# Two of the four weight sums of a paired step computed on GpSimd

## What is computed

```
def swiglu(x, w_gate, w_up, w_down):
    return (jax.nn.silu(x @ w_gate) * (x @ w_up)) @ w_down
...
        f = swiglu(rms_norm_2(x, g[0]), ffn_w_gate[layer, 0], ffn_w_up[layer, 0], ffn_w_down[layer, 0])
        x = x + 0.5 * rms_norm_2(f, g[1])
```

## Time and profile before

| | us |
|---|---|
| median of 3 runs (1793.16 to 1794.82) | 1794.06 |
| the profiled execution | 1793.34 |
| its span, from the first to the last instruction | 1790.4 |
| TensorE busy | 1754.3 |
| VectorE busy | 1389.7 |
| ScalarE busy | 995.0 |
| GpSimd busy | 58.1 |

### The profile page before, as it was taken

The page is one execution under the profiler, slowest core; times in us unless marked ns, Lnnn a source line. Parts: engine busy times, 40 slices in busy tenths (PEclk is TensorE's granted clock), DMA queues, the critical chain, the costliest instruction groups (busy, mean ns, idle before and its releaser), DMA issues.

```text
span 1790.4 us, 25225 instructions
## 1 busy us (share of the span) xinstructions
PE 1754.3 (98%) x10314; PEld 1482.6 (83%) x10314; DVE 1389.7 (78%) x1646; ACT 995.0 (56%) x1206; POOL 58.1 (3%) x98
## 2 busy tenths in 40 slices
PE   9999999999999999999999999999999999999998
PEld 8998898888888887787898988778877878787877
DVE  5349877788898898978498779886897667879784
ACT  5446653577777676645452355555555456656453
POOL 0040000000000001000000000000100010010000
PEclk9999999999999999999999999999999999999999
DMA  9343344699899897373442016527443745234631
GB/s 383 118 165 136 119 148 149 240 359 351 337 351 354 334 372 293 123 280 139 190 152 108 27 53 230 225 83 312 180 170 136 305 143 187 72 141 150 273 147 76
DMA packets 51379, 363.01 MB, mean 203 GB/s; under 512 B 5697, under 2 KB 5825, under 8 KB 8642
## 3 DMA queue, kind: packets, MB, share of 16 engines
q1 hardware_dynamic: 50976, 359.24, 52.6%
q10 hardware_dynamic: 290, 2.17, 0.3%
HBM read 360.34 MB, written 1.05 MB: 202 GB/s over the span
## 4 chain that ended last, share of the span: by engine, by line
PE 79%; DVE 15%; ACT 3%; issue 1%; DMA 1%; POOL 0%; DVEq 0%; POOLq 0%; ACTq 0%
PE bank L2866 8%; PE bank L3424 4%; PE bank L3426 4%; PE bank L3425 4%; PE bank L3451 3%; PE bank L3449 3%; PE bank L3450 3%; PE bank L3278 3%; PE bank L3280 3%; PE bank L3279 3%; DVE w_a L1718 3%; PE bank L3483 3%; PE bank L2924 3%; PE bank L3484 2%; PE bank L3485 2%; PE bank L3295 2%
## 5 line engine op out<-in xcount | busy, mean ns | idle before, releaser
L1718 DVE TENSOR_TENSOR w_a<-ring,w_a 128x2048 fp32r<-128x2048 f32 x220 | 500.4, 2287 | 132.5 <-ACT w_a L994 131.8
L994 ACT ACTIVATE w_a<-ring 128x2048 fp32r<-128x2048 f32 x219 | 416.2, 1913 | 121.4 <-PE bank L3451 42.1
L1718 DVE TENSOR_TENSOR w_b<-ring,w_b 128x2048 fp32r<-128x2048 f32 x63 | 144.1, 2287 | 29.3 <-ACT w_b L994 29.2
L994 ACT ACTIVATE w_b<-ring 128x2048 fp32r<-128x2048 f32 x63 | 120.5, 1912 | 36.2 <-PE bank L3426 17.8
L2866 PE MATMUL bank<-h,w_a 128*128 128x256 f32 x1040 | 137.3, 285 | 1.0 <-DVE ring_lo L1823 1.0
L2866 PEld LDWEIGHTS bank<-h,w_a 128*128 128x128 f32 x1040 | 128.8, 191 | 4.1 <-issue 3.0
L3449 PE MATMUL bank<-w_a,hid 128*128 128x512 f32 x280 | 109.9, 393 | 0.0
L3451 PE MATMUL bank<-w_a,hid 128*128 128x512 f32 x280 | 109.2, 390 | 0.0
L3450 PE MATMUL bank<-w_a,hid 128*128 128x512 f32 x280 | 109.0, 389 | 0.0
L3424 PE MATMUL bank<-w_a,h 128*128 128x512 f32 x240 | 95.0, 396 | 0.5 <-DVE w_a L1718 0.5
L3426 PE MATMUL bank<-w_a,h 128*128 128x512 f32 x240 | 93.7, 390 | 0.0
(11 more groups left out here) (648 smaller groups left out, 4201.1 us busy)
## 6 DMA issues: line engine op xcount, KB each, us to landing
ring<-in_stream SPq DMA_DIRECT2D x330, 1024.0 KB, 5.3
G<-in_gains SPq DMA_DIRECT2D x14, 512.0 KB, 7.8
cmp_area<-in_cmp_w ACTq DMA_DIRECT2D x1, 2048.0 KB, 11.3
sm<-in_small SPq DMA_DIRECT2D x1, 1582.0 KB, 12.0
con<-in_consts SPq DMA_DIRECT2D x1, 1032.0 KB, 15.9
X<-in_x SPq DMA_DIRECT2D x2, 512.0 KB, 4.0
out_x<-X SPq DMA_DIRECT2D x4, 256.0 KB, 2.0
sm<-in_small SPq DMA_DIRECT2D x1, 730.5 KB, 22.5
```

The costliest lines, as they stand in the source:

```text
L994: act.activation(w_slot(unit)[:, 0, :], ring[:, unit % RING, :], ACT.Copy).then_inc(S("w_hi"), 1)
L1718: dve.tensor_tensor(w_slot(unit)[:, 1, :], ring[:, unit % RING, :], w_slot(unit)[:, 0, :].bitcast(FP32), ALU.subtract).then_inc(S("w_lo"), 1)
```

## The change

t3 and t1 move to GpSimd, which runs its own `weight_sums` in each network: t3 as soon as b12 and b22 have landed. t1 is now computed inside the pair, as b22 - t2 (t2 is b22 - b12 + b11), when t2 is made and m6 is done. VectorE's t2 waits for GpSimd's t3. The high half of t1 on ScalarE waits for GpSimd's t1, and so does the load into b11's place, which followed m6 before; the load into b22's place waits for t1 too. The low half of t2 is written to `w_sum_lo` (the tile `y_2`) instead of `ring_lo`. GpSimd's count is kept in the semaphore `ffn_pool`, in which the sparse network's steps count first (`m_silu` before).

```diff
--- before.py
+++ after.py
@@ -668,9 +668,10 @@
...
-        PAIR_DVE = ["t1", "t3", "t2", "t4", "t2_lo", "u2", "t4_lo", "u3", "c21", "t1_lo", "w", "c12", "c22"]
+        PAIR_DVE = ["t2", "t4", "t2_lo", "u2", "t4_lo", "u3", "c21", "t1_lo", "w", "c12", "c22"]
         FFN_DVE = ["x_raw", "s1", "s2", "s3", "s4", "s_lo"] + [f"{step}_{i}" for i in range(len(PAIRS)) for step in PAIR_DVE]
         FFN_ACT = ["s_hi"] + [f"{step}_{i}" for i in range(len(PAIRS)) for step in ("t2_hi", "m1", "t4_hi", "t1_hi")]
+        FFN_POOL = [f"{step}_{i}" for i in range(len(PAIRS)) for step in ("t3", "t1")]
         FFN_PE = [f"{step}_{i}" for i in range(len(PAIRS)) for step in ("m6", "m7", "m4", "m5")]
 
         def ffn_at(steps, name, step):
@@ -737,10 +738,12 @@
                 return "sums_0", NB[name] - (NB[name] > NB["ffn0"])
             return "unit_used", D_UNITS[of] + (3 * STEPS[of] if of in STEPS else SQUARE)
 
+        SUMMED = {}
         for name in FFNS:
             for i, s in enumerate(PAIRS):
-                b11, b21, _, _ = pair_units(name, s)
-                RELEASE[b11] = ("ffn_pe", ffn_at(FFN_PE, name, f"m6_{i}"))
+                b11, b21, _, b22 = pair_units(name, s)
+                SUMMED[b22] = ffn_at(FFN_POOL, name, f"t1_{i}")
+                RELEASE[b11] = ("ffn_pool", ffn_at(FFN_POOL, name, f"t1_{i}"))
                 RELEASE[b21] = ("ffn_pe", ffn_at(FFN_PE, name, f"m4_{i}"))
 
         def tops_done(name, s):
@@ -818,6 +821,8 @@
                 if u >= RING:
                     name, count = RELEASE.get(u - RING, ("unit_used", u - RING + 1))
                     sp.wait_ge(S(name), count)
+                    if u - RING in SUMMED:
+                        sp.wait_ge(S("ffn_pool"), SUMMED[u - RING])
                 sp.dma_start(ring[:, u % RING, :], unit_at(u)).then_inc(S(f"unit{u % RING}"), 16)
 
             def load_gain(row, place):
@@ -939,18 +944,33 @@
                 src, dst = dst, src
 
 
+            def weight_sums(name):
+                for i, s in enumerate(PAIRS):
+                    b11, _, b12, b22 = pair_units(name, s)
+                    for b in (b12, b22):
+                        pool.wait_ge(S(f"unit{b % RING}"), 16 * (b // RING + 1))
+                    pool.tensor_tensor(ring[:, b12 % RING, :], ring[:, b22 % RING, :], ring[:, b12 % RING, :], ALU.subtract)\
+                        .then_inc(S("ffn_pool"), 1)
+                    pool.wait_ge(S("ffn_dve"), ffn_at(FFN_DVE, name, f"t2_{i}"))
+                    pool.wait_ge(S("ffn_pe"), ffn_at(FFN_PE, name, f"m6_{i}"))
+                    pool.tensor_tensor(w_sum, ring[:, b22 % RING, :], ring[:, b11 % RING, :], ALU.subtract).then_inc(S("ffn_pool"), 1)
+
             post_power("moe")
-            for name in ("ffn0", "ab"):
-                post_power(name)
+            post_power("ffn0")
+            weight_sums("ffn0")
+            post_power("ab")
...
-            for name in ("ffn1", "ffn2", "c"):
+            for name in ("ffn1", "ffn2"):
                 post_power(name)
-            for name in ("ffn3", "end"):
-                post_power(name)
+                weight_sums(name)
+            post_power("c")
+            post_power("ffn3")
+            weight_sums("ffn3")
+            post_power("end")
 
 
         @block.scalar
@@ -1348,7 +1368,7 @@
                     if s == 0:
                         act.wait_ge(S("route_dve"), AT["rc_ok"])
                     act.wait_ge(S("unit_used"), m0 + place_A("moe", s) + 2)
-                    act.activation(sil_m[:, :], bank[4][:, 0:UC], ACT.Silu, scale=rc[:, 6 * i + 4:6 * i + 5]).then_inc(S("m_silu"), 1)
+                    act.activation(sil_m[:, :], bank[4][:, 0:UC], ACT.Silu, scale=rc[:, 6 * i + 4:6 * i + 5]).then_inc(S("ffn_pool"), 1)
                     if s:
                         split_at(3 * s + 3)
                     act.wait_ge(S("ffn_pe"), s + 1)
@@ -1412,6 +1432,7 @@
                     act.wait_ge(S("unit_used"), b21 + 1)
                     silu_of(bank[4], 0)
                     split_at(3 * s + 4)
+                    act.wait_ge(S("ffn_pool"), ffn_at(FFN_POOL, name, f"t1_{i}"))
                     act.wait_ge(S("ffn_pe"), ffn_at(FFN_PE, name, f"m4_{i}"))
                     act.activation(sum_hi[:, :], w_sum, ACT.Copy).then_inc(S("ffn_act"), 1)
                     act.wait_ge(S("ffn_dve"), ffn_at(FFN_DVE, name, f"c21_{i}"))
@@ -2296,7 +2317,7 @@
 
                 for s in range(SPARSE_STEPS):
                     i, j = s // GRP_STEPS, s % GRP_STEPS
-                    dve.wait_ge(S("m_silu"), s + 1)
+                    dve.wait_ge(S("ffn_pool"), s + 1)
                     e = 6 * i + j // 2
                     dve.scalar_tensor_tensor(mid_m[:, s % 2, :], bank[4][:, UC:2 * UC], rc[:, e:e + 1], sil_m[:, :], ALU.mult, ALU.mult)\
                        .then_inc(S("ffn_dve"), 1)
@@ -2361,20 +2382,10 @@
                     own("s2")
                     dve.tensor_tensor(x_sum[:, 3], a12, x_sum[:, 1], ALU.subtract).then_inc(S("ffn_dve"), 1)
 
-                def weight_sums(i, s):
-                    b11, b21, b12, b22 = pair_units(name, s)
-                    raw = [ring[:, b % RING, :] for b in (b11, b21, b12, b22)]
-                    if i:
-                        dve.wait_ge(S("ffn_pe"), ffn_at(FFN_PE, name, f"m5_{i - 1}"))
-                    dve.wait_ge(S(f"unit{b11 % RING}"), 16 * (b11 // RING + 1))
-                    dve.wait_ge(S(f"unit{b12 % RING}"), 16 * (b12 // RING + 1))
-                    dve.tensor_tensor(w_sum, raw[2], raw[0], ALU.subtract).then_inc(S("ffn_dve"), 1)
-                    dve.wait_ge(S(f"unit{b22 % RING}"), 16 * (b22 // RING + 1))
-                    dve.tensor_tensor(raw[2], raw[3], raw[2], ALU.subtract).then_inc(S("ffn_dve"), 1)
-
                 def more_weight_sums(i, s):
                     b11, b21, b12, _ = pair_units(name, s)
-                    own(f"t3_{i}")
+                    dve.wait_ge(S("ffn_pool"), ffn_at(FFN_POOL, name, f"t3_{i}"))
+                    dve.wait_ge(S(f"unit{b11 % RING}"), 16 * (b11 // RING + 1))
                     dve.tensor_tensor(ring[:, b11 % RING, :], ring[:, b12 % RING, :], ring[:, b11 % RING, :], ALU.add).then_inc(S("ffn_dve"), 1)
                     own(f"t2_{i}")
                     dve.tensor_tensor(ring[:, b21 % RING, :], ring[:, b21 % RING, :], ring[:, b11 % RING, :], ALU.subtract)\
@@ -2440,13 +2451,11 @@
                     hid_left(s - 1, range(0, 2))
                     if s + 2 == PAIRS[0]:
                         x_whole()
-                    if ahead is not None:
-                        weight_sums(ahead, s + 1)
                     split_at(3 * s + 3)
                     hid_made(s, 1)
                     if ahead is not None:
                         more_weight_sums(ahead, s + 1)
-                        ring_left(f"t2_hi_{ahead}", pair_units(name, s + 1)[0])
+                        sum_left(f"t2_hi_{ahead}", w_sum_lo, ring[:, pair_units(name, s + 1)[0] % RING, :])
                     split_at(3 * s + 4)
                     if s + 2 == PAIRS[0]:
                         x_sums()
@@ -3496,7 +3505,7 @@
                     product(4, own[0], whole[0], True).then_inc(S("unit_used"), 1)
                     turn(s - 1, range(0, 2))
                     sum_ready(f"t2_lo_{i}")
-                    product(7, both[1], (sum_hi[:, :], ring_lo[:, b11 % RING, :]), True).then_inc(S("ffn_pe"), 1)
+                    product(7, both[1], (sum_hi[:, :], w_sum_lo), True).then_inc(S("ffn_pe"), 1)
                     pe.wait_ge(S("ffn_act"), ffn_at(FFN_ACT, name, f"m1_{i}"))
                     lo_ready(b21)
                     product(4, own[1], whole[1], False).then_inc(S("unit_used"), 1)
```

## The result

| | us |
|---|---|
| median before, 4 runs | 1793.61 |
| median after, 4 runs (1818.48 to 1822.93) | 1822.64 |
| ratio, 95% interval | 1.0159 (1.0144 to 1.0174) |
| span of the profiled execution after (the 1818.48 one) | 1816.6 |

The change costs 29 us. The prediction had its sign and its place, but 9.2 us, and the time lies outside the range that ended at 1812. In the changed kernel the lines of VectorE are some 20 higher than before, those of TensorE 9 higher. First the page: span and busy times, to be read against the earlier trace rows.

What follows compares the result with a forecast made beforehand. The prediction took TensorE as the bound, waiting on VectorE's queue ahead of a pair. It set 18.6 us lost at m4 against 9.4 gained at m6: +9.2, from 1794.06 to 1803.3 us, range 1792 to 1812.

Steps and rivals of the forecast that it cites:

- t1's duration D: GpSimd, inside each pair: t1's 2048 elements take 3.78 us; the price is 8 us for each us of D.
- either way hidden: GpSimd, ahead of the pair: t3 ends at 745.2 or 748.4, before t2 started, and so costs nothing.
- gain at m6: TensorE's wait for t2's low half, ahead of m6: t2 comes 1.18 us earlier, eight times, 9.4 us gained.
- What bounds the kernel: TensorE, busy 1754.3 of 1790.4 us; the only wait in reach is m6's, 9.6 us in eight times.
- D - 1.45: Lateness of m4 per pair as a function of t1's duration D; 2.33 us at D of 3.78.
- The place and the mechanism: Inside the pair, b22's low half waits 2.56 us for t1's SBUF port; m4 2.33 late, 18.6 us lost in all.
- What is moved to t1's end: The load into b11's place, issued at about 763.3, not 759.32; its delay stays hidden, with 0.8 us left at `hid`.
- Sum: Whole kernel: 8 x (2.33 - 1.18) = +9.2 us, 1803.3 on the median.
- The rival with D above 4.1: GpSimd needs longer than 4.1 us for t1: 5.6 us more per 0.7 us, 1809 at 4.5; chance 0.16.
- The remark that VectorE has 2.2 us less work ahead of the pair: VectorE's queue: 2.2 us less work ahead of the pair, paid for by 2.3 us inside it.

Runs made afterwards that it cites:

- memset kernel: The changed kernel with t1 left out and replaced on GpSimd by three memsets of its tile, 1.81 us each; 1800.21 us, ratio 1.0038.
- filled kernel: The changed kernel with 12 more matmuls per pair, into a bank nobody reads, ahead of TensorE's wait for m4; 1813.7 us, ratio 1.0114.
- last experiment: The kernel before, all on VectorE, with t1 of the second pairs alone moved ahead of the pair's `hid`; 1791.05 us, ratio 0.9989.
- t3 held: The changed kernel with t3 held on GpSimd until the pair's `hid_left` is done; 1829.23 us, ratio 1.0204.

## Why the prediction was wrong, point by point

Three terms of the prediction's sum failed. t1's duration D was mis-sized. t3, "either way hidden", was not: it was given no price. And nothing was counted for TensorE's clock behind the new wait. With D right the forecast is 1809.4, still inside the range of 1792 to 1812; t3 and the smaller gain at m6 add 4.6 to it, and the clock some 9.

- **What bounds the kernel: right; the gain at m6: right in kind, too large.** 9.4 us were counted and 7.2 measured. In the first pairs it was 0.93 to 0.96 in place of 1.18; with t3 back on VectorE it was 1.16 to 1.18 in three of the four. In the second pairs the wait was 1.06 and not 1.4, so 0.86 was all that there was.
- **t3 is hidden: wrong.** This step looked only at when t3 ends, and asked who waits for it. It took for granted that GpSimd would stand behind VectorE's line 2392. t3 started 0.19 us before it, took the port, and VectorE waited, 6.70 us for 2.28. That is 2.4 us at the down product, and some 0.6 at m6, which is part of the gain that was missing there.
- **t1's duration: the term mis-sized.** 3.78 us by proportion from a row of 1084 elements; 4.57 to 4.6 measured. The row was of another kind of operands, 20% cheaper (1.99 against 2.47 us alone). With 4.6 the prediction's own formula, D - 1.45, gives 3.15 at m4; 3.09 was measured. That is 8 x 0.76 = 6.1 us. The Trainium skill's figure of 4497 ns (GPSIMD Engine Reference, "Elementwise — side-by-side cycle accounting") was better than the row: it was 4.49 with GpSimd alone.
- **The place and the mechanism: right.** b22's low half behind c12, then c22, then m4, eight times, 3.32 us of waiting in the first pair's row. The Trainium skill, SBUF — State Buffer, "Who interferes with whom", says that a GpSimd operation that only writes does not contend, and that issue order decides who waits. The trace agrees with both, with the memset of 1.81 beside 2.28, and with `x_left`, 6.70 when t3 was first and 2.28 when it was not. In the memset kernel's first pair the two start within 0.02 us of each other (t3 at 739.59, `x_left` at 739.61), and there it is t3 that is recorded longer, 6.79: starts as close as that do not tell who has the port.
- **What is moved to t1's end: right here,** but only under the later m4. The memset kernel shows the bill when m4 is on time: 1.4 to 1.9 us at each turn. In the changed kernel the first pair's `hid` ends at 778.81 and the turn comes at 779.43, so 0.6 us are left where the prediction had 0.8.
- **The clock: missing from the sum,** 8 to 9 us by the filled kernel. A new wait of 2.3 us, eight times, was forecast without a word on what TensorE does after it. In the kernel before, waits at the pairs are 1.4 us at most and no clock is lost there. No run has a wait of exactly the forecast 2.3 us; those of 2.5 us (t1 in two instructions) cost the clock in five of eight pairs.
- **Sum.** 9.2 forecast; +6.1 for t1's duration, +2.2 for the gain at m6, +2.4 for t3 at the down product, +9 for the clock make 28.9, and 29.0 was measured; the 9 is read from medians, and so good to 1 us. The rival with D above 4.1 (1809 at 4.5) was the right one on D. The remark that VectorE has 2.2 us less work ahead of the pair counts one of the two operations that left, 4.4 us; the sum does not use it. The range failed since it took the unknown duration for the only unknown.

## What to carry to other kernels

In these kernels a GpSimd operation that reads SBUF was paid for by VectorE with that part of its length that lay over VectorE's own work on two SBUF operands. It was twice as long as VectorE's 2.28 us, so moving it only pays where it falls into idle time of VectorE, and such an idle time can take the work itself, as the last experiment did. To price an operation, take a row with the same kind of operands, and not only of the nearest size. Where an edit makes TensorE wait as long as here, 2.5 us and more, add to its price the matmuls that may run at half clock behind it, 1.7 us each time here.

## What the runs showed of the hardware

- tensor_tensor on GpSimd, float32, 128 partitions: 0.18 us + 2.10 ns an element from two tiles (4.49 us for 2048); 1.99 in place of 2.47 us for 1084 when the two operands are one tile a column apart. In the loaded kernel the 2048 take 4.57 to 4.62, counted from when the operation has the port.
- With VectorE and GpSimd operations that read SBUF queued against each other, the port changed hands at the end of each instruction: with t1 in two pieces VectorE waited 1.07 us, then GpSimd, then VectorE again 1.85. The time spent waiting is inside the row of the instruction that waits (5.60 and 6.70 us for 2.28), and no idle time is shown.
- The granted clock fell to 0.50 late in or right after some waits of 2.9 us (3 of 8 in the changed kernel's profile, 7 of 8 with t1 alone on GpSimd, 6 of 8 with t3 held), after some of 2.5 us (5 of 8 with t1 in two pieces), at all eight of 3.5 to 3.8 us with t3 alone, and after none of 0.7 or 1.4 us at the pairs. Length is not all: outside the pairs the kernel before loses the clock at 1448.2, right behind a wait of 1.8 us. Why one wait costs the clock and the next does not was not settled.
